# The first transfer of x in two column pieces, each row tile rounded by itself

## The chip, the core and the metric

The kernel runs on one core of one Trainium2 chip. The metric is the device time of one execution, in microseconds (us). The kernel before takes 770.45 us (median of three runs, 770.39 to 770.49).

## The reference, cut to what matters

The layer normalises x (256 tokens by 2048), multiplies it with one wide input projection, runs two attention branches, gates and merges them, projects the result and adds x. Only the first step bears on the change:

```python
def rms_norm(x, gain, eps=NORM_EPS):
    xf = x.astype(jnp.float32)
    y = xf * lax.rsqrt(jnp.mean(xf * xf, axis=-1, keepdims=True) + eps)
    return (y * gain.astype(jnp.float32)).astype(x.dtype)

for l in range(DEPTH):
    h = rms_norm(x, norm_gain[l])
    proj = jnp.einsum('bsd,dn->bsn', h, w_in[l])
    (qa, ka, va, ga, qi, ki, wi, qb, kb, vb, gb, ma, mb) = jnp.split(proj, offsets, axis=-1)
    ...
    merged = jax.nn.sigmoid(ma) * ya + jax.nn.sigmoid(mb) * yb
    x = x + jnp.einsum('bsd,de->bse', merged, w_out[l])
```

`apply_rope` turns the heads by angles, which are the token positions times 64 fixed frequencies.

## The kernel before

**Split products.** Every float32 operand of a matmul is taken as two parts: `hi`, the value rounded to the matmul format (fp32r), and `lo`, the value minus `hi`. A product is three matmuls: hi by hi, lo by hi and hi by lo.

**x.** The program gets x also as `x_columns`, which is x transposed, 128 features to a k-tile, 16 k-tiles of 256 tokens (two row tiles of 128). Ahead of the tiles stand the norm gains (16 columns, `gainT`) and the rotary frequencies (64 columns, `freq`). The SBUF tile `xt` holds all of it. `hT_hi` is x times gain, rounded; `hT_lo` is what is left. In `hT_lo` the rounded columns 64 to 255 of a k-tile are kept once more for packed matmuls (`x_hi_again`, line 1015).

**Units.** Weights are streamed: a unit is two k-tiles of one column chunk, 512 columns wide at most, in a ring of four slots (`raw`, `hi`, `lo`). SyncE (SP) issues the loads, ScalarE (ACT) makes `hi`, VectorE (DVE) makes `lo`, TensorE (PE) multiplies. From unit 4 on, SP waits before a load until DVE has made the `lo` of the unit four places before (line 497 waits, line 499 issues), since the slot is free then. The first three units (`EARLY = 3`) are loaded and split in two halves j = 0 and j = 1, one k-tile each; `FIRST_UNITS` gives the order of the first 24: unit 0 is 336 columns wide, units 1 to 4 are 512, unit 5 is 336.

**The start.** The order of each engine is written out by hand. ACT issues the first transfer of `xt` (line 1003: gains, frequencies and k-tile 0, 336 columns), then loads its function table, rounds the weights of unit 0, rounds columns 64 to 255 of k-tile 0 once more (line 1015, after `x_landed[0]`), and goes on with units 1 and 2 (line 1020). SP issues meanwhile six loads of weights and the next k-tile of x (lines 490 and 482). DVE waits for `x_landed[0]`, makes `hT_hi` of k-tile 0 (line 1453), its `hT_lo` (line 1323), and then the `lo` of the weights (line 1463 for halves, line 1332 for whole units). PE runs 14 matmul records of zeros as a warm-up (line 810). Its real work starts in `rounded_part`: hi by `hT_hi` for the second row tile (line 774) and, in unit 0, for the first (line 776), then by `hT_lo` (lines 778, 780, 784); `low_part` adds `lo` by `hT_hi` (lines 794, 795). Units 1 and 2 use packed rows in place of line 776, which take part of the first row tile. GpSimd (POOL) needs `freq` and the positions to make the rotary angles.

The semaphores of the start are `x_landed[0]` (the transfer), `x_hi_first`, `x_lo_first` and `x_again_first` (k-tile 0 rounded, its rest, its second copy), `hi_first` and `lo_first` (weights, half j = 0), and `hi_ready`, `lo_ready` (half j = 1 and all later units).

Of the kernel before, what the change touches and what calls it, by code (L numbers as in the profile page):

```python
# [30 lines left out]
P = 128  # L31
D = 2048
S = 256
LAST_PIECES = ((0, slice(0, 512)), (1, slice(0, 256)), (1, slice(256, 512)))
RT = S // P
KT = D // P
HD = 128
# [9 lines left out]
BLOCK = 32  # L47
X_CUTS = (0, 1, 2, 4, 6, 8, 10, 12, 14, 16)
X_FRONT = KT + HD // 2
EARLY = 3  # L50
SINES_AT = 12
X_OWN_AFTER = ((3, 2), (3, 4), (3, 6), (4, 0))
# [123 lines left out]
def chunk_bank(c):  # L176

    return {0: 0, 1: 2, 2: 6, 3: 4, 4: 2, 6: 4}.get(c, 2 * ((c + 1) % 2)) if isinstance(c, int) else 2 * ((c + 1) % 2)


def build_layer(nc, x, x_columns, positions, w_in, a_q_gain, a_k_gain, b_q_gain, b_k_gain,
# [4 lines left out]
    with ExitStack() as ctx:  # L186
        place = [-(-nc.sbuf_base // 64) * 64]

        def sb(name, shape, dt=F32, at=None):

            size = 4
            for n in shape[1:]:
                size *= n
            offset = place[0] if at is None else at
            if at is None:
                place[0] += -(-size // 64) * 64
                assert place[0] <= nc.sbuf_usable_end, (name, place[0])
            return nc.alloc_sbuf_tensor_at(name, shape, dt, offset=offset)

        def sem(name):  # L200
            return ctx.enter_context(nc.semaphore(name))
# [6 lines left out]
        hT_hi = sb("hT_hi", [P, KT, S], F32R)  # L208
# [4 lines left out]
        def lo_rows(k, r):  # L213
            return hT_lo[:, k, r * LO_STEP:r * LO_STEP + P]
# [24 lines left out]
        m = sb("m", [P, RT, 2 * D])  # L239
        m_r = sb("m_r", [P, RT, 2 * D], F32R, at=m_at)  # L240
        xt = sb("xt", [P, X_FRONT + KT * S], at=m_at)
        gainT, freq = xt[:, 0:KT], xt[:, KT:X_FRONT]

# [16 lines left out]
            return QK_GAINS[n - C_QK] % 2 == 0  # L262

        def x_tile(k):
            return xt[:, X_FRONT + k * S:X_FRONT + (k + 1) * S]

# [152 lines left out]
        T0, S0 = 4, 6  # L421


        x_landed = [sem(f"x_landed_{i}") for i in range(len(X_CUTS) - 1)]
        phases_landed = sem("phases_landed")
        consts_landed = sem("consts_landed")
# [9 lines left out]
        hi_ready, lo_ready, unit_done = sem("hi_ready"), sem("lo_ready"), sem("unit_done")  # L436
        raw_first = [sem(f"raw_first_{i}") for i in range(EARLY)]
        hi_first, lo_first = sem("hi_first"), sem("lo_first")
        x_hi_first, x_lo_first, x_again_first = sem("x_hi_first"), sem("x_lo_first"), sem("x_again_first")
# [39 lines left out]
        def _(sp):  # L479
            def load_x(j):  # L480
                at = slice(X_FRONT + X_CUTS[j] * S, X_FRONT + X_CUTS[j + 1] * S)
                sp.dma_start(xt[:, at], x_columns[:, at]).then_inc(x_landed[j], 16)
# [5 lines left out]
            def load_first(u, j):  # L488
                c, i = FIRST_UNITS[u]
                sp.dma_start(raw[:, u, j, 0:FIRST_W[c]],  # L490
                             w_in[0][(2 * i + j) * P:(2 * i + j + 1) * P, FIRST_COLS[c]:FIRST_COLS[c] + FIRST_W[c]]
                             ).then_inc((raw_first[u], raw_landed[u])[j], 16)

            def load(slot, u, weights, k0, col, width=CW):

                if not isinstance(u, int) or u >= RING:
                    sp.wait_ge(lo_ready, u - (RING - 1))
                src = weights[0][k0 * P:(k0 + 2) * P, bass.ds(col, width)].rearrange("(k p) n -> p k n", p=P)
                sp.dma_start(raw[:, slot, :, 0:width], src).then_inc(raw_landed[slot], 16)
# [17 lines left out]
            for j in range(2):  # L517
                if j == 1:
                    load_x(1)
                for u in range(EARLY):  # L520
                    load_first(u, j)
            for u in range(EARLY, 3 * CK):
                c, i = FIRST_UNITS[u]
                if c == 0:
                    load_x(i + 1)
                load(u % RING, u, w_in, 2 * i, FIRST_COLS[c], FIRST_W[c])
                if u == EARLY + 1:
                    sp.dma_start(pos_i[:, :], positions).then_inc(phases_landed, 16)
# [219 lines left out]
        def _(pe):  # L748
# [16 lines left out]
            def rounded_part(u, j):  # L765

                c, unit_k = FIRST_UNITS[u]
                k, bank, width = 2 * unit_k + j, chunk_bank(c), FIRST_W[c]
                o_0, o_1 = ps[:, bank, 0:width], ps[:, bank + 1, 0:width]
                w_hi = hi[:, u % RING, j, 0:width]  # L770
                first = k == 0
                pe.wait_ge(hi_first if j == 0 and u < EARLY else hi_ready, u + 1)
                pe.wait_ge(x_hi_first if k == 0 else split_hi, unit_k + 1)
                mm(o_1, hT_hi[:, k, P:S], w_hi, start=first, stop=False)  # L774
                if c >= PACKED:
                    mm(o_0, hT_hi[:, k, 0:P], w_hi, start=first, stop=False)  # L776
                pe.wait_ge(x_lo_first if k == 0 else split_lo, unit_k + 1)
                mm(o_1, lo_rows(k, 1), w_hi, start=False, stop=False)  # L778
                if c >= PACKED:
                    mm(o_0, lo_rows(k, 0), w_hi, start=False, stop=False)  # L780
                else:
                    if k == 0:
                        pe.wait_ge(x_again_first, 1)
                    mm(o_0, packed_rows(k), w_hi, start=first, stop=False)  # L784

            def low_part(u, j):
# [5 lines left out]
                last = k == KT - 1  # L792
                pe.wait_ge(lo_first if j == 0 and u < EARLY else lo_ready, u + 1)
                mm(o_1, hT_hi[:, k, P:S], w_lo, start=False, stop=last)  # L794
# [204 lines left out]
        @block.scalar  # L999
        def _(act):  # L1000
            activation = nc.scalar.activation
            at = slice(0, X_FRONT + X_CUTS[1] * S)
            act.dma_start(xt[:, at], x_columns[:, at]).then_inc(x_landed[0], 16)

            def x_hi(t):
                for j in range(len(X_CUTS) - 1):
# [10 lines left out]
            def early_hi(u, j):  # L1017
                act.wait_ge((raw_first[u], raw_landed[u])[j], 16)
                width = FIRST_W[FIRST_UNITS[u][0]]
                activation(hi[:, u, j, 0:width], raw[:, u, j, 0:width],  # L1020
                           ACT.Copy).then_inc((hi_first, hi_ready)[j], 1)
# [114 lines left out]
                ins.then_inc(indexT_ready, 1)  # L1136

            early_hi(0, 0)
            act.wait_ge(x_landed[0], 16)
            x_hi_again(0).then_inc(x_again_first, 1)  # L1140
            for u in range(1, EARLY):
# [15 lines left out]
            for c in range(2, C_V):  # L1157
                for i in range(CK - RING if c == 2 else 0, CK):
                    at = c * CK + i
# [42 lines left out]
            for c in range(C_V, C_O):  # L1202
                for i in range(CK):
                    u = c * CK + i
                    if i == 0:
                        if c == C_V:
                            qk_group(C_QK + QK_GROUPS - 1)
                        elif c <= C_G:
                            at = (c - 1 - C_V) * CW
                            chunk_to(c - 1, lambda r: v[:, r, at:at + CW])  # L1210
                        elif c <= C_M:
                            at = (c - 1 - C_G) * CW
                            chunk_to(c - 1, lambda r: g[:, r, at:at + CW], ACT.Silu)
                        else:


                            at = (c - 1 - C_M) * CW
# [84 lines left out]
            at = slice(3 * CW + cols.start, 3 * CW + cols.stop)  # L1302
# [5 lines left out]
        def _(dve):  # L1308
            tt, stt, ts = nc.vector.tensor_tensor, nc.vector.scalar_tensor_tensor, nc.vector.tensor_scalar
# [139 lines left out]
                    ins = tt(by_blocks(of_four(n, part, m_r)), columns_of(r), rounded, ALU.subtract)  # L1449
                ins.then_inc(qk_lo_ready, 1)  # L1450

            dve.wait_ge(x_landed[0], 16)
            ts(hT_hi[:, 0, :], x_tile(0), gainT[:, 0:1], None, ALU.mult).then_inc(x_hi_first, 1)  # L1453
            dve.wait_ge(x_hi_first, 1)
            x_lo_tile(0).then_inc(x_lo_first, 1)
            for j in range(2):
                if j == 1:
# [12 lines left out]
            for c in range(2, C_V):  # L1470
                for i in range(CK - RING if c == 2 else 0, CK):
                    at = c * CK + i
# [105 lines left out]
            for c in range(C_V, C_O):  # L1578
                for i in range(CK):
# [46 lines left out]
                    if u in VB_LO:  # L1626
                        n = VB_LO.index(u)
                        at = slice(n * CW, (n + 1) * CW)
# [36 lines left out]
                    if U_B + 8 <= u < U_OGT + 8:  # L1665
# [5 lines left out]
                        if step == (6 if h == B_HEADS - 1 else 7):  # L1671
# [3 lines left out]
                            for t in range(RT):  # L1675
                                at = A_W + h * 2 * HD
# [114 lines left out]
```

## Time and profile before

| what | value |
|---|---|
| median of the runs | 770.45 us |
| the profiled execution's own time | 770.51 us |
| its span | 768.7 us |
| PE busy | 764.8 us, 99% of the span |
| DVE busy | 516.9 us, 67% |
| ACT busy | 431.1 us, 56% |
| granted TensorE clock | full in all 40 slices |
| DMA | 176.80 MB, mean 230 GB/s |

The span runs from the first to the last instruction; 1.8 us of the execution lie outside it. A busy PE says that matmuls follow one another; weight loads for it (PEld) run beside them. "Idle before" is the time in which an engine did nothing ahead of an instruction, and the name behind the arrow is what ended that.

### The profile page before, as it was taken

Reading aid. Unit: us, or ns where it says so; the run is one execution under the profiler, and the core shown is the slowest. Engines: PE = TensorE matmul, PEld = TensorE weight load, DVE = VectorE, ACT = ScalarE, POOL = GpSimd, SP = SyncE. Lnnn points to the kernel's source line nnn. Section 1 sums busy time; section 2 is a strip of 40 time slices with the busy share of each in tenths; the row PEclk is TensorE's granted clock in tenths of the full one; section 3 lists DMA queues with packets and bytes.
Section 4 is the critical chain, followed back from the end, with each engine's and each line's share of the span. In section 5 each row is a group of like instructions: output and inputs, shape, how many; then the busy total and the mean of one; then the engine's idle time right before and its main releaser. Section 6 shows DMA issues by size and latency. Waiting matters only on the chain.

```text
span 768.7 us, 10429 instructions
## 1 busy us (share of the span) xinstructions
PE 764.8 (99%) x3568; PEld 643.8 (84%) x3568; DVE 516.9 (67%) x724; ACT 431.1 (56%) x710; POOL 135.8 (18%) x225
## 2 busy tenths in 40 slices
PE   9999999999999999999999999999999999999998
PEld 8899988888888888888888888888888888888887
DVE  6768788888776755678656665767465567765553
ACT  6855756676663745555656565455576334444331
POOL 4412533322221000000212222312110011110000
PEclk9999999999999999999999999999999999999999
DMA  8988889998888675666866768767767888887553
GB/s 294 318 258 276 264 245 291 276 254 266 245 245 243 187 200 167 193 192 172 240 207 197 222 192 270 234 185 222 224 208 224 302 230 240 246 242 230 198 183 122
DMA packets 89612, 176.80 MB, mean 230 GB/s; under 512 B 7616, under 2 KB 15424, under 8 KB 89312
## 3 DMA queue, kind: packets, MB, share of 16 engines
q1 hardware_dynamic: 80752, 152.06, 65.8%
q0 software_dynamic: 8528, 23.87, 10.9%
q8 instruction: 25, 0.41, 0.2%
q10 hardware_dynamic: 288, 0.30, 0.1%
q14 instruction: 19, 0.16, 0.1%
HBM read 162.18 MB, written 14.02 MB: 229 GB/s over the span
## 4 chain that ended last, share of the span: by engine, by line
PE 99%; DMA 0%; DVE 0%; issue 0%
PE ps L760 29%; PE ps L762 29%; PE ps L761 29%; PE ps L774 1%; PE ps L778 1%; PE ps L794 1%; PE ps L795 1%; PE ps L784 1%; PE ps L860 0%; PE ps L963 0%; PE ps L962 0%; PE ps L961 0%; DMA xt<-in_x_columns 0%; PE ps L780 0%; PE ps L776 0%; PE ps L861 0%
## 5 line engine op out<-in xcount | busy, mean ns | idle before, releaser
L1332 DVE TENSOR_TENSOR lo<-raw,hi 128x1024 fp32r<-128x1024 f32 (+2 forms) x277 | 331.2, 1202 | 230.1 <-ACT hi L1041 229.3
L1041 ACT ACTIVATE hi<-raw 128x1024 fp32r<-128x1024 f32 (+2 forms) x277 | 286.3, 1038 | 291.5 <-PE ps L762 254.7
L760 PE MATMUL ps<-hi,hT_hi 128*128 128x512 f32 (+1 forms) x880 | 339.9, 386 | 0.0
L761 PE MATMUL ps<-lo,hT_hi 128*128 128x512 f32 (+1 forms) x880 | 339.0, 385 | 0.0
L762 PE MATMUL ps<-hi,hT_lo 128*128 128x512 f32 (+1 forms) x880 | 339.0, 385 | 0.0
L762 PEld LDWEIGHTS ps<-hi,hT_lo 128*128 128x128 f32 x880 | 165.2, 188 | 32.1
L760 PEld LDWEIGHTS ps<-hi,hT_hi 128*128 128x128 f32 x880 | 165.2, 188 | 31.5
L761 PEld LDWEIGHTS ps<-lo,hT_hi 128*128 128x128 f32 x880 | 165.2, 188 | 31.3
L760 PE MATMUL ps<-hi,ogT_hi 128*128 128x512 f32 x128 | 49.8, 389 | 0.0
L761 PE MATMUL ps<-lo,ogT_hi 128*128 128x512 f32 x128 | 49.8, 389 | 0.0
L762 PE MATMUL ps<-hi,ogT_lo 128*128 128x512 f32 x128 | 49.8, 389 | 0.0
L704 POOL DMA_DIRECT2D probs<-work x12 | 6.8, 567 | 173.3 <-DVE work L1536 173.3
L711 POOL DMA_DIRECT2D work<-probs x48 | 26.1, 550 | 53.1 <-DMA probs<-work 53.1
L761 PEld LDWEIGHTS ps<-lo,ogT_hi 128*128 128x128 f32 x128 | 24.0, 188 | 5.0
L760 PEld LDWEIGHTS ps<-hi,ogT_hi 128*128 128x128 f32 x128 | 24.0, 188 | 5.0
L762 PEld LDWEIGHTS ps<-hi,ogT_lo 128*128 128x128 f32 x128 | 24.0, 188 | 5.0
L688 POOL DMA_DIRECT2D v<-turned x32 | 17.5, 554 | 28.4 <-DMA turned<-swapped 24.7
L1182 ACT ACTIVATE work<-work,small 128x128 f32<-128x128 f32 (+1 forms) x32 | 14.3, 447 | 13.4 <-DVE small L1507 13.4
L1102 ACT ACTIVATE roped<-stage 128x128 f32<-128x128 f32 x64 | 18.9, 296 | 0.3
L774 PE MATMUL ps<-hi,hT_hi 128*128 128x512 f32 (+1 forms) x48 | 17.7, 369 | 0.3 <-DVE hT_hi L1453 0.3
L604 POOL TENSOR_TENSOR small<-small,half 128x8 f32<-128x8 f32 (+1 forms) x13 | 17.8, 1369 | 1.1
L738 POOL DMA_DIRECT2D turned<-swapped x4 | 2.2, 559 | 88.1 <-DVE swapped L1718 88.1
(199 smaller groups left out, 665.1 us busy)
## 6 DMA issues: line engine op xcount, KB each, us to landing
raw<-in_w_in SPq DMA_DIRECT2D x190, 512.0 KB, 4.5
raw<-in_w_out SPq DMA_DIRECT2D x32, 512.0 KB, 4.2
raw<-in_w_o_a SPq DMA_DIRECT2D x16, 512.0 KB, 5.9
raw<-in_w_o_b SPq DMA_DIRECT2D x16, 512.0 KB, 4.2
raw<-in_w_in SPq DMA_DIRECT2D x16, 384.0 KB, 4.9
turned<-swapped POOLq DMA_DIRECT2D x12, 512.0 KB, 3.3
v<-turned POOLq DMA_DIRECT2D x32, 128.0 KB, 5.8
raw<-in_w_in SPq DMA_DIRECT2D x7, 336.0 KB, 4.6
```

Of the source, the lines that this page charges most:

```text
L604: return tt(out, mean, half[:, 0:width], ALU.pow)
L688: pool.dma_start(to.rearrange("j (q n) -> j q n", q=P // BLOCK), turned_rows[c]).then_inc(turned_back, 16)
L711: pool.dma_start(to.rearrange("j (q n) -> j q n", q=P // BLOCK), rows[c]).then_inc(probs_back, 16)
L760: mm(o, a_hi, w_hi[:, j], start=first and j == 0, stop=False)
L761: mm(o, a_hi, w_lo[:, j], start=False, stop=False)
L762: ins = mm(o, a_lo, w_hi[:, j], start=False, stop=j == 1 and last)
L774: mm(o_1, hT_hi[:, k, P:S], w_hi, start=first, stop=False)
L778: mm(o_1, lo_rows(k, 1), w_hi, start=False, stop=False)
L1041: activation(hi[:, slot, :, 0:width], raw[:, slot, :, 0:width], ACT.Copy).then_inc(hi_ready, 1)
L1102: ins = activation(roped[:, r, at], stage[:, r, at], ACT.Square, accum_out=ss_h[:, j:j + 1])
L1182: ins = activation(probs[buf][:, at], masked[buf][:, at], ACT.Exp, scale=SCALE, bias=neg_max[:, j:j + 1], accum_out=sum_p[:, j:j + 1])
L1332: tt(lo[:, slot, :, 0:width], raw[:, slot, :, 0:width], hi[:, slot, :, 0:width].bitcast(F32), ALU.subtract).then_inc(lo_ready, 1)
```

## The change

The layout of `x_columns` becomes: frequencies (64 columns), k-tile 0 (256 columns), gains (16 columns), then the other k-tiles at the places they had. ACT now issues two transfers in place of one. Each piece has a semaphore of its own, `x_half_landed` for the second row tile (columns 192 to 319) with the gains (320 to 335), and `x_landed[0]` for the frequencies (0 to 63) with the first row tile (64 to 191). `X_HALF = 192` is where they meet. The piece with the second row tile is issued first; it is 144 columns (72 KB), the other 192 columns (96 KB).

DVE rounds k-tile 0 in two instructions of 128 columns, each after its own piece, and goes on with `hT_lo` when both are done. PE waits for the first before line 774's matmul and for both before line 776's. ACT waits for both before its second rounding. POOL waits for `x_landed[0]` as before.

```diff
+X_FIRST = HD // 2
+X_HALF = X_FIRST + P
...
-        gainT, freq = xt[:, 0:KT], xt[:, KT:X_FRONT]
+        gainT, freq = xt[:, X_FIRST + S:X_FRONT + S], xt[:, 0:X_FIRST]
...
         def x_tile(k):
-            return xt[:, X_FRONT + k * S:X_FRONT + (k + 1) * S]
+            first = X_FIRST if k == 0 else X_FRONT + k * S
+            return xt[:, first:first + S]
...
+        x_half_landed = sem("x_half_landed")
...
                 if c >= PACKED:
+                    if k == 0:
+                        pe.wait_ge(x_hi_first, 2)
                     mm(o_0, hT_hi[:, k, 0:P], w_hi, start=first, stop=False)
...
-            at = slice(0, X_FRONT + X_CUTS[1] * S)
-            act.dma_start(xt[:, at], x_columns[:, at]).then_inc(x_landed[0], 16)
+            for at, landed in ((slice(X_HALF, X_FRONT + S), x_half_landed), (slice(0, X_HALF), x_landed[0])):
+                act.dma_start(xt[:, at], x_columns[:, at]).then_inc(landed, 16)
...
             early_hi(0, 0)
+            act.wait_ge(x_half_landed, 16)
             act.wait_ge(x_landed[0], 16)
             x_hi_again(0).then_inc(x_again_first, 1)
...
-            dve.wait_ge(x_landed[0], 16)
-            ts(hT_hi[:, 0, :], x_tile(0), gainT[:, 0:1], None, ALU.mult).then_inc(x_hi_first, 1)
-            dve.wait_ge(x_hi_first, 1)
+            for rows, landed in ((slice(P, S), x_half_landed), (slice(0, P), x_landed[0])):
+                dve.wait_ge(landed, 16)
+                ts(hT_hi[:, 0, rows], x_tile(0)[:, rows], gainT[:, 0:1], None, ALU.mult).then_inc(x_hi_first, 1)
+            dve.wait_ge(x_hi_first, 2)
             x_lo_tile(0).then_inc(x_lo_first, 1)
...
-    x_columns = _np.concatenate([_np.asarray(inputs["norm_gain"])[0].reshape(KT, P).T,
-                                 _np.broadcast_to(freqs, (P, HD // 2)),
-                                 _np.asarray(inputs["x"])[0].T.reshape(KT, P, S).transpose(1, 0, 2).reshape(P, KT * S)],
-                                axis=1)
+    x_tiles = _np.asarray(inputs["x"])[0].T.reshape(KT, P, S).transpose(1, 0, 2).reshape(P, KT * S)
+    x_columns = _np.concatenate([_np.broadcast_to(freqs, (P, HD // 2)), x_tiles[:, 0:S],
+                                 _np.asarray(inputs["norm_gain"])[0].reshape(KT, P).T, x_tiles[:, S:]], axis=1)
```

The start of ACT's own program before, where `xt` is x with gains and frequencies, `hi` and `raw` the weights rounded and as loaded:

```order
L1003 DMA xt<-in_x_columns 128x336
L1020 ACT_TABLE_LOAD
L1020 ACTIVATE hi<-raw 128x336 [waits raw_first_0]
L1015 ACTIVATE hT_lo<-xt 128x64 [waits x_landed_0]
L1020 ACTIVATE hi<-raw 128x512 [waits raw_first_1]
```

And of the changed kernel, the same place:

```order
L1011 DMA xt<-in_x_columns 128x144
L1011 DMA xt<-in_x_columns 128x192
L1028 ACT_TABLE_LOAD
L1028 ACTIVATE hi<-raw 128x336 [waits raw_first_0]
L1023 ACTIVATE hT_lo<-xt 128x64 [waits x_landed_0,x_half_landed]
L1028 ACTIVATE hi<-raw 128x512 [waits raw_first_1]
```

One issue stands more ahead of the table load, and the second rounding of x waits for both pieces; nothing else has moved.

The start of DVE's program before, where `hT_hi` and `hT_lo` are the two parts of x and `lo` the rest of the weights:

```order
L1453 TENSOR_SCALAR hT_hi<-xt 128x256 [waits x_landed_0]
L1323 SCALAR_TENSOR_TENSOR hT_lo<-xt,hT_hi 128x2x128 [waits x_hi_first]
L1463 TENSOR_TENSOR lo<-raw,hi 128x336 [waits hi_first]
L1463 TENSOR_TENSOR lo<-raw,hi 128x512 [waits hi_first] x2
L1323 SCALAR_TENSOR_TENSOR hT_lo<-xt,hT_hi 128x2x128 [waits split_hi]
```

And of the changed kernel:

```order
L1463 TENSOR_SCALAR hT_hi<-xt 128x128 [waits x_half_landed]
L1463 TENSOR_SCALAR hT_hi<-xt 128x128 [waits x_landed_0]
L1332 SCALAR_TENSOR_TENSOR hT_lo<-xt,hT_hi 128x2x128 [waits x_hi_first]
L1473 TENSOR_TENSOR lo<-raw,hi 128x336 [waits hi_first]
L1473 TENSOR_TENSOR lo<-raw,hi 128x512 [waits hi_first] x2
L1332 SCALAR_TENSOR_TENSOR hT_lo<-xt,hT_hi 128x2x128 [waits split_hi]
```

The rounding of k-tile 0 is cut in two, and what follows has its place and its waits as before.

## Rows read from the trace of the kernel before

**Rows 1.** The page: busy us, share of the span and instructions of each engine.
```profile
PE 764.8 (99%) x3568; PEld 643.8 (84%) x3568; DVE 516.9 (67%) x724; ACT 431.1 (56%) x710; POOL 135.8 (18%) x225
```

**Rows 2.** Waits in the whole span: engine, line, releaser, total us, times, longest.
```profile
PEld ps L774 <- ACT hi L1041: 0.5, 1, 0.5
```

**Rows 3.** Chain of waits, 0 to 6 us: start, length, what.
```profile
0.74 3.11 DMA xt<-in_x_columns
...
3.88 0.36 DVE hT_hi L1453
4.24 0.14 issue
4.38 0.43 PE ps L774
```

**Rows 4.** Timeline of ACT, ACTq being its DMA issues: start, length, instruction.
```profile
0.74 0.40 ACTq L1003 DMA_DIRECT2D xt<-in_x_columns  x1
...
3.68 0.48 ACT L1020 ACTIVATE hi<-raw 128x336 fp32r<-128x336 f32 x1 [1.22 <-DMA raw<-in_w_in]
4.07 0.33 ACT L1015 ACTIVATE hT_lo<-xt 128x64 fp32r<-128x64 f32 x1
4.46 1.30 ACT L1020 ACTIVATE hi<-raw 128x512 fp32r<-128x512 f32 x2
...
12.50 1.06 ACT L1041 ACTIVATE hi<-raw 128x1024 fp32r<-128x1024 f32 x1 [1.74 <-DMA raw<-in_w_in]
```

**Rows 5.** Timeline of DVE, 3 to 7.3 us.
```profile
4.26 0.49 DVE L1323 SCALAR_TENSOR_TENSOR hT_lo<-xt,hT_hi 128x256 fp32r<-128x256 f32 x1
4.67 0.50 DVE L1463 TENSOR_TENSOR lo<-raw,hi 128x336 fp32r<-128x336 f32 x1
...
5.12 1.36 DVE L1463 TENSOR_TENSOR lo<-raw,hi 128x512 fp32r<-128x512 f32 x2
...
5.79 0.69 DVE L1463 TENSOR_TENSOR lo<-raw,hi 128x512 fp32r<-128x512 f32 x1
...
6.84 0.50 DVE L1463 TENSOR_TENSOR lo<-raw,hi 128x336 fp32r<-128x336 f32 x1
```

**Rows 6.** Timeline of PE around 13.4 us.
```profile
12.96 0.39 PE L794 MATMUL ps<-lo,hT_hi 128*128 128x512 f32 x1
13.19 0.39 PE L795 MATMUL ps<-lo,hT_lo 128*128 128x512 f32 x1
13.62 0.50 PE L774 MATMUL ps<-hi,hT_hi 128*128 128x512 f32 x1
13.96 0.40 PE L778 MATMUL ps<-hi,hT_lo 128*128 128x512 f32 x1
```

**Rows 7.** DMA issues between 0 and 0.9 us: KB each, us to landing.
```profile
raw<-in_w_in SPq DMA_DIRECT2D x1, 168.0 KB, 2.9
```

**Rows 8.** The same, issues between 1.5 and 2.9 us.
```profile
raw<-in_w_in SPq DMA_DIRECT2D x2, 256.0 KB, 3.3
...
raw<-in_w_in SPq DMA_DIRECT2D x1, 168.0 KB, 3.3
```

**Rows 9.** SP's timeline, and unit 4's time to landing.
```profile
2.60 1.38 SPq L490 DMA_DIRECT2D raw<-in_w_in  x3
...
7.37 0.38 SPq L499 DMA_DIRECT2D raw<-in_w_in  x1
...
raw<-in_w_in SPq DMA_DIRECT2D x1, 512.0 KB, 5.1
```

**Rows 10.** DMA queues, 2 to 4 us: packets, MB, share of 16 engines.
```profile
q1 hardware_dynamic: 289, 0.46, 66.2%
q10 hardware_dynamic: 144, 0.17, 25.5%
```

**Rows 11.** Stretches: us; busy PE, PEld, DVE, ACT, POOL; clock, DMA share, GB/s.
```profile
10.00:12.00 2.00, 2.00 (x10) 1.67 (x9) 1.93 (x3) 0.76 (x1) 0.00 (x0) 1.00 0.95 302
...
14.00:244.00 230.00, 230.00 (x1087) 198.15 (x1086) 182.95 (x230) 150.13 (x308) 72.56 (x104) 1.00 0.89 265
```

## The prediction

> **What bounds the kernel now.** I began with the page's first part. PE is busy 764.8 of 768.7 us [rows 1], so only time in which PE waits can be won or lost, unless its own work changes, and no matmul is added or taken away. The second view is that of the waits over the whole span. For PE it has, besides a pause ahead of the index scores that no engine ends, only places in the first 14 us: line 774's first matmul waits for DVE's `hT_hi`, and a later weight load of the same line, for unit 4, waits for ACT's `hi` [rows 2]. The table of stretches says the same: from 14 to 244 us PE is busy 230.00 of 230.00 us at the full granted clock [rows 11]. So whatever the change does must reach past 14 us, or it is gone.
>
> The third view, the chain of waits, shows the first place: the transfer of x is issued at 0.74 and lands 3.11 us later at 3.85, DVE rounds it until 4.24, and PE starts at 4.38 [rows 3]. The timeline of PE shows the second: matmuls follow one another by 0.23 us (12.96 to 13.19), so the next was due at 13.42, but the next starts at 13.62 and its follower only at 13.96, 0.34 behind instead of 0.23 [rows 6]. That is 0.20 us idle plus 0.11 us of restart. ACT explains it: its `hi` of unit 4 began at 12.50 after 1.74 us of waiting for the weights, and took 1.06 [rows 4]. Those weights were issued at 7.37 and landed 5.1 us later [rows 9]. This second place is the bound that counts. A start of PE that comes earlier makes it wait longer there, and a start up to 0.20 us later is swallowed there.
>
> **When the two pieces land.** The whole 168 KB took 3.11 us. SP's 168 KB of the same moment took 2.9, its 256 KB 3.3 [rows 7, 8]. That is 0.4 us for 88 KB, 0.0045 us per KB. The first piece (72 KB, 96 less) then takes 3.11 - 0.44 = 2.67 us from 0.74 and lands at 3.41. The second is issued one issue later; an issue takes 0.40 us [rows 4], with the gap to the next some 0.43, so at 1.17. It has 96 KB (72 less): 3.11 - 0.33 = 2.78 us, landing at 3.95. Bounds: were time proportional to bytes it would be 1.17 + 3.11 x 96/168 = 2.95; at the slower early load's 3.3 us, 4.47 [rows 8]. I take 3.95, since two early loads of different size give the slope. So the second piece lands about 0.10 us later than the whole did.
>
> **DVE, part by part.** Before, it began at 3.88, and `hT_lo` at 4.26. The first rounding now runs from 3.44 and is over before the second piece is there. For 128 columns no row exists: 336 columns take 0.50 and 512 take 0.69 [rows 5], 0.0011 us per column, so the cut of 128 takes 0.14 off the 0.36 of 256 columns [rows 3], which leaves 0.22 (bounds: half of 0.36, 0.18; all of it, 0.36). Then: 3.95 + 0.03 + 0.22 + 0.03 = 4.23 for the start of `hT_lo`, 0.03 earlier than 4.26. With the bounds of the rounding it is 4.19 to 4.37.
>
> Does a gain there go on? `lo` of unit 0 would start at 4.64 instead of 4.67. But `lo` of unit 1 starts at 5.12 [rows 5], and the `hi` it needs comes from ACT: rounding at 4.46, two of 512 in 1.30 us, so the first is over at about 5.10 [rows 4]. ACT's chain from 3.68 has no idle time up to there and begins with the landing of unit 0's weights. The second `lo` of this kind, at 5.79, stands right behind ACT's end at 4.46 + 1.30 = 5.76. From there DVE goes on to `lo` of unit 0's second half, 6.84 to 7.34, which lets SP issue unit 4 at 7.37 [rows 5, 9]. So ACT carries the date of unit 4, and an earlier DVE start is worth nothing.
>
> **ACT.** The second issue moves ACT's table load back by 0.43. The 1.22 us wait for weights that ended at 3.68 [rows 4] hides it; uncovered it would cost the 0.43. At 4.07 ACT needs both pieces: free if the second lands by 4.04. DVE, by the sum above, tolerates 4.02. Both margins over 3.95 are about 0.08 us; a landing L later than that moves ACT, DVE and the issue of unit 4 by L - 4.03. At 4.47 that is 0.44.
>
> **PE.** The first matmul needs the second row tile (3.44 + 0.22 = 3.66) and `hi` of unit 0, ready at 3.68 + 0.48 = 4.16, which is the later. With the 0.14 between release and start [rows 3] it starts at 4.30, 0.08 earlier than 4.38. The added wait ahead of line 776 (both roundings, 4.20) is met by then. Behind it stand the `hT_lo` matmuls, that need DVE's 4.23 + 0.49, and the low part, that needs 5.14: there the gain is down to 0.03 us, and at 13.42 it is nothing. If the added wait does hold, the whole in-order queue of PE stands behind it, again with 0.20 us of cover. Had the 0.08 survived to the end, 770.4 would be the time.
>
> **POOL and SP.** POOL needs `freq` only together with the positions, which SP issues after unit 4's weights, at over 7.37 us [rows 9]: nothing. No issue of SP is moved.
>
> **More packets.** The x queue had 144 packets in its 25.5% of 2 us x 16 engines, 57 ns each at 1.2 KB; the other queue 289 in 66.2%, 73 ns at 1.6 KB [rows 10]. The line through both gives 11 ns without bytes. A second transfer adds as many packets as one has, 144: 144 x 11 / 16 = 0.10 us for each engine (bounds: none, or all 57 ns fixed, 0.51). The engines are the bound until unit 4 lands, but not wholly: their share is 0.95 between 10 and 12 us [rows 11]. I take half, 0.05 us, on the landing of unit 4, and from there to the end, as PE never waits again.
>
> **The sum.** PE's start -0.08, of which 0 is left; unit 4's issue 0; its landing +0.05. The profiled execution would go from 770.51 to 770.56, 0.06 above the median, so the forecast is 770.5 us.
>
> **Two rules weighed.** The transfer's time against its size is 3.11 us for 168 KB here. The Trainium skill (DMA: Bandwidth & Descriptors, Anatomy of one DMA — SWDGE (gpsimd) path) gives about 2.0 us fixed and the bytes over 436 GB/s, measured on POOL's path. By the slope of that rule the second piece saves 0.17 us and lands at 1.17 + 2.94 = 4.11, over the threshold: an estimate of +0.08 us, where the rows give 0. On the order between queues, both show bytes in the same 2 us, in shares 25.5 and 66.2% [rows 10]. The same page (Queues, rings and completion order) says that an engine takes turns between queues, packet by packet; the trace agrees, and it speaks against the third rival.
>
> **The rivals.**
> 1. *Fixed cost per transfer (a little slower).* If 96 KB take nearly what 168 KB took, the second piece lands at up to 1.17 + 3.11 = 4.28: 0.25 us late for ACT and DVE, unit 4 issued at 7.62. It decides from 4.03. With the packets 770.45 + 0.25 + 0.05 = 770.75. For it: 168 KB issued later by SP took 3.3 us, no less than 256 KB [rows 8]. Against: it ran among more traffic.
> 2. *Weights earlier (a little faster).* 96 of the 168 KB of x come 0.43 us later, so unit 0's weights meet less company; 98 thousand bytes at the 0.63 MB in 2 us seen there [rows 10] are 0.31 us. ACT could start at 3.37, but its second instruction waits for 3.95 + 0.03 and not 4.07: 0.09 of it is left, and 0.07 after DVE. Time 770.4.
> 3. *The second piece behind SP's loads (slower).* SP issues two loads of 256 KB and one of x right behind its first, and the second halves from 2.60 on [rows 9]. If the second piece is served only after all up to the first of those, it lands with that, at 2.60 + 3.3 = 5.90 [rows 8]: 5.90 - 4.03 = 1.87 us on ACT, DVE and unit 4, which carries it past PE's cover. Time 772.3. A change that can be measured needs a landing past 5.57.
> 4. *It does not do what it says.* The halves are there one by one, but PE's first matmul waits for `hi` of unit 0. That is inside the forecast.
>
> **How the numbers follow.** Forecast 0.62, rival 1 0.18, rival 2 0.14, rival 3 0.03, anything not named 0.03. A difference under 0.2%, 1.54 us, can't be told from no change here. Only rival 3 is past it, and half of the unnamed on either side: faster 0.02, within 0.2% 0.94, slower 0.04. The range takes in rivals 1 and 2, the packets' upper bound (0.51) and some tenths for transfers that interleave otherwise: 770.1 to 771.0.
>
> **What would show it.** Two transfers on ACT's queue, landing near 3.4 and 3.95; DVE's `hT_lo` between 4.19 and 4.30; PE's first matmul near 4.30, waiting for ACT and not for DVE; the idle time near 13.4 still there, 0.20 to 0.3 us; unit 4's `hi` between 12.4 and 12.7; PE without idle time after it. I am wrong if PE's wait at 13.4 vanishes, if the landing of unit 4 moves by over 0.3 us, or if the second piece lands after 4.3.

## The result, and the profile after

The changed kernel takes 772.17 us (median of 22 runs, 770.71 to 773.22), the kernel before, run beside it, 770.43 us (22 runs, 770.15 to 771.61). The ratio of the two, taken over all runs and not from the medians (these alone give 1.0023), is 1.0017, 95% interval 1.0011 to 1.0023: slower, by more than the measurement is uncertain and by about 0.2%. In the experiments below, too, the ratio stands beside the median and is not worked out from it. The median of 772.17 lies outside the predicted range of 770.1 to 771.0.

The times of the changed kernel are two groups with nothing between 771.33 and 772.09: 8 runs at 770.71 to 771.33 and 14 at 772.09 to 773.22. Of the kernel before 21 of 22 are at or under 770.94. The profiled execution, 772.63 us with a span of 770.8, is one of the upper group, and so is the median; of the lower group no execution was profiled.

The page has PE 2.2 us busier, with the same number of matmuls, which answers to [rows 1]; part 3 has 432 packets on the queue of x's first transfer, where before it has 288:

```profile
PE 767.0 (99%) x3568; PEld 645.9 (84%) x3568; DVE 517.2 (67%) x725; ACT 431.2 (56%) x710; POOL 135.8 (18%) x225
...
q10 hardware_dynamic: 432, 0.30, 0.1%
```

PE does the same work and needs longer for it. The waits of PE and PEld in the whole span (engine, line, releaser, total us, times, longest) have changed place against [rows 2]; the wait for unit 4's weights is gone, and those that another engine ends are all in the first 6 us:

```profile
PE ps L784 <- DVE hT_hi L1463: 0.3, 1, 0.3
...
PEld ps L784 <- DVE hT_hi L1463: 0.7, 1, 0.7
...
PEld ps L786 <- DVE hT_lo L1332: 0.2, 1, 0.2
PEld ps L780 <- ACT hi L1028: 0.2, 1, 0.2
```

The chain of waits up to 7 us (start, length, what) answers to [rows 3]. The second piece is issued at 1.18, lands 3.46 us later, at 4.64, and PE's second matmul starts at 5.00:

```profile
0.74 0.41 ACTq L1011
...
1.18 3.46 DMA xt<-in_x_columns
...
4.66 0.30 DVE hT_hi L1463
...
5.00 0.65 PE ps L784
5.65 0.52 PE ps L786
```

DVE's first rounding starts when the first piece is there, near 3.6. ACT starts on unit 0's weights earlier than in [rows 4] and then waits for the second piece of x:

```profile
3.61 0.28 DVE L1463 TENSOR_SCALAR hT_hi<-xt 128x128 fp32r<-128x128 f32 x1 [3.61 <-DMA xt<-in_x_columns]
```

```profile
3.42 0.48 ACT L1028 ACTIVATE hi<-raw 128x336 fp32r<-128x336 f32 x1 [0.48 <-DMA raw<-in_w_in]
4.72 0.35 ACT L1023 ACTIVATE hT_lo<-xt 128x64 fp32r<-128x64 f32 x1 [0.82 <-DMA xt<-in_x_columns]
```

The timeline of PE has the loss itself:

```profile
4.04 0.62 PE L780 MATMUL ps<-hi,hT_hi 128*128 128x336 f32 x1
5.00 0.65 PE L784 MATMUL ps<-hi,hT_hi 128*128 128x336 f32 x1 [0.35 <-DVE hT_hi L1463]
...
6.25 0.48 PE L802 MATMUL ps<-lo,hT_hi 128*128 128x336 f32 x1
6.53 0.48 PE L803 MATMUL ps<-lo,hT_hi 128*128 128x336 f32 x1
6.81 0.63 PE L780 MATMUL ps<-hi,hT_hi 128*128 128x512 f32 x1
7.24 0.63 PE L786 MATMUL ps<-hi,hT_lo 128*128 128x512 f32 x1
...
8.94 0.63 PE L780 MATMUL ps<-hi,hT_hi 128*128 128x512 f32 x1
9.37 0.53 PE L786 MATMUL ps<-hi,hT_lo 128*128 128x512 f32 x1
9.74 0.40 PE L792 MATMUL ps<-hi,hT_lo 128*128 128x512 f32 x1
...
10.43 0.32 PE L780 MATMUL ps<-hi,hT_hi 128*128 128x336 f32 x1
...
16.14 0.39 PE L786 MATMUL ps<-hi,hT_lo 128*128 128x512 f32 x1
```

Read the distances between starts. Matmuls of 336 columns follow by 0.28 us and those of 512 by 0.43, that is 1.2 columns per ns, the lower of TensorE's two levels (1.2 GHz). From 9.74 on those of 512 follow by 0.23, 2.2 columns per ns, the upper level (2.4 GHz). The matmul at 9.37, with 0.53 us between the 0.63 of one level and the 0.40 of the other, is where the pace rose. The kernel before does its 512-column matmuls 0.23 apart from the first one on, and the short 0.31 us of its second matmul, at 4.64, say that it has the upper level by then:

```profile
4.64 0.31 PE L776 MATMUL ps<-hi,hT_hi 128*128 128x336 f32 x1
...
5.64 0.39 PE L774 MATMUL ps<-hi,hT_hi 128*128 128x512 f32 x1
5.87 0.40 PE L778 MATMUL ps<-hi,hT_lo 128*128 128x512 f32 x1
...
6.80 0.39 PE L774 MATMUL ps<-hi,hT_hi 128*128 128x512 f32 x1
...
7.93 0.31 PE L774 MATMUL ps<-hi,hT_hi 128*128 128x336 f32 x1
```

The ledger follows from these two timelines. PE's second matmul is 0.36 us late (5.00 against 4.64), unit 1's first 1.17 (6.81 against 5.64), unit 2's first 2.14 (8.94 against 6.80), unit 0's second half 2.50 (10.43 against 7.93). Then the pace is equal, and at unit 4 the idle time and restart of [rows 6] are not there any more, which gives 0.32 back: its second matmul is at 16.14 instead of 13.96, 2.18 late. The span is 2.1 us longer.

The column of granted clock does not tell this. It says 1.00 in both kernels for 5.00 to 9.30 us. The count in brackets behind PE's busy time does: 22 matmuls that fall at least in part into that stretch before, and 11 after. First before, then after (columns as in [rows 11]):

```profile
5.00:9.30 4.30, 4.30 (x22) 3.70 (x22) 3.70 (x7) 3.79 (x10) 0.00 (x0) 1.00 1.06 358
```

```profile
5.00:9.30 4.30, 4.30 (x11) 3.57 (x12) 4.11 (x8) 3.79 (x10) 0.00 (x0) 1.00 1.02 349
```

The load of unit 4, which the prediction took for the bound, was issued later and landed earlier, against [rows 9] and [rows 4]. SP's issue, its time to landing and ACT's rounding of it:

```profile
7.93 0.38 SPq L505 DMA_DIRECT2D raw<-in_w_in  x1
...
raw<-in_w_in SPq DMA_DIRECT2D x1, 512.0 KB, 3.6
```

```profile
11.61 1.06 ACT L1049 ACTIVATE hi<-raw 128x1024 fp32r<-128x1024 f32 x1 [0.48 <-DMA raw<-in_w_in]
```

### The profile page after: what moved, and what is told of

It reads as the page before. It is cut to its first block, busy times and chain, and to the rows that moved or that the text cites. A ratio compares the mean times of both kernels' runs of the same rounds, so it can differ in the third digit from the quotient of the medians.

```text
span 770.8 us, 10432 instructions
## 1 busy us (share of the span) xinstructions
PE 767.0 (99%) x3568; PEld 645.9 (84%) x3568; DVE 517.2 (67%) x725; ACT 431.2 (56%) x710; POOL 135.8 (18%) x225
## 4 chain that ended last, share of the span: by engine, by line
PE 99%; DMA 0%; DVE 0%; ACTq 0%; issue 0%
PE ps L766 29%; PE ps L767 29%; PE ps L768 29%; PE ps L786 1%; PE ps L802 1%; PE ps L803 1%; PE ps L780 1%; PE ps L792 1%; PE ps L868 0%; DMA xt<-in_x_columns 0%; PE ps L969 0%; PE ps L971 0%; PE ps L970 0%; PE ps L784 0%; PE ps L788 0%; PE ps L869 0%
## 5 line engine op out<-in xcount | busy, mean ns | idle before, releaser
L768 PE MATMUL ps<-hi,hT_lo 128*128 128x512 f32 (+1 forms) x880 | 339.1, 385 | 0.0
L1191 ACT ACTIVATE work<-work,small 128x128 f32<-128x128 f32 (+1 forms) x32 | 14.2, 446 | 13.4 <-DVE small L1517 13.4
L786 PE MATMUL ps<-hi,hT_lo 128*128 128x512 f32 (+1 forms) x48 | 18.3, 381 | 0.0
```

Source lines behind the costliest of these rows:

```text
L768: ins = mm(o, a_lo, w_hi[:, j], start=False, stop=j == 1 and last)
L1191: ins = activation(probs[buf][:, at], masked[buf][:, at], ACT.Exp, scale=SCALE, bias=neg_max[:, j:j + 1], accum_out=sum_p[:, j:j + 1])
```

## The experiments

Two theories stood at the start. **A**: zeros end at 4.10 us, and PE then has too little work, one lone matmul until 5.0; the rise of its pace to the upper level, which else comes about then, stays out until 9.4 to 9.7, and the slow matmuls are the loss. **B**: the second piece is late and delays DVE, ACT and the load of unit 4; the pace has no part in it. All kernels ran beside the kernel before, in three sets: its median was 770.52 us beside the first four, 770.46 beside the next four and 770.60 beside the last three.

**More warm-up in the changed kernel.**

```diff
-WARM_UP = 7
+WARM_UP = 9
```

> The changed kernel with 9 zero matmuls (18 records) of warm-up in place of 7, so that zeros run until about 5.06 us instead of 4.10. Theory A (PE's idle time behind the warm-up keeps the matmuls of 4.0 to 9.4 us at 1.2 GHz, and these slow matmuls are the loss): the first real matmuls run at 2.4 GHz (336 columns 0.15 us apart), the second mode of the times is gone, 770.4 to 770.9 us. Theory B (the late second piece delays DVE, ACT and the load of unit 4, the clock plays no part): the landing stays late, 771.7 us or more, since PE starts no earlier.

Measured: 770.87 us (770.67 to 773.16, 11 runs; ratio 1.0010, 1.0001 to 1.0019), one run above 771.44. The second piece was still late, at 4.5, and PE's weight loads waited 0.4 us for its rounding and 0.3 us for `hT_lo`, but the real matmuls ran at the upper level. The zero records start 0.2 us apart up to 4.10 and the last two of them 0.11 to 0.12 apart, so the pace rose while the zeros ran, about 0.2 us ahead of the first real matmul:

```profile
3.68 0.92 PE L818 MATMUL ps<-const-float32-0.0 128*128 128x128 f32 x5
4.36 0.40 PE L780 MATMUL ps<-hi,hT_hi 128*128 128x336 f32 x1
4.88 0.42 PE L784 MATMUL ps<-hi,hT_hi 128*128 128x336 f32 x1
...
6.24 0.39 PE L780 MATMUL ps<-hi,hT_hi 128*128 128x512 f32 x1
6.47 0.40 PE L786 MATMUL ps<-hi,hT_lo 128*128 128x512 f32 x1
```

1.3 of the 1.7 us between the medians went with two more zero matmuls and no other edit. A holds. What is left, 0.35 us over the 770.52 of the kernel before beside it, is the most that B alone is worth.

**Less warm-up in the kernel before.**

```diff
-WARM_UP = 7
+WARM_UP = 5
```

> The kernel before, one transfer, with 5 zero matmuls of warm-up, so that zeros end near 3.15 us and PE idles some 1.2 us before 4.38. Nothing is late but the warm-up. Theory A: slow matmuls at the start in most executions, 772 us or more. Theory B: no change, 770.4 us.

Measured: 772.64 us (771.70 to 773.39, 7 runs; ratio 1.0026, 1.0014 to 1.0037). Nothing in it is late but the end of the zeros. x landed at 3.9 as before, and PE had 14 matmuls in the stretch from 5.00 to 9.30 where the kernel before has 22:

```profile
4.42 0.62 PE L774 MATMUL ps<-hi,hT_hi 128*128 128x336 f32 x1 [1.17 <-DVE hT_hi L1453]
...
9.64 0.63 PE L794 MATMUL ps<-lo,hT_hi 128*128 128x512 f32 x1
10.07 0.58 PE L795 MATMUL ps<-lo,hT_lo 128*128 128x512 f32 x1
10.49 0.31 PE L774 MATMUL ps<-hi,hT_hi 128*128 128x336 f32 x1
```

**The transfer split, the rounding not.**

```diff
-            for rows, landed in ((slice(P, S), x_half_landed), (slice(0, P), x_landed[0])):
-                dve.wait_ge(landed, 16)
-                ts(hT_hi[:, 0, rows], x_tile(0)[:, rows], gainT[:, 0:1], None, ALU.mult).then_inc(x_hi_first, 1)
-            dve.wait_ge(x_hi_first, 2)
+            dve.wait_ge(x_half_landed, 16)
+            dve.wait_ge(x_landed[0], 16)
+            ts(hT_hi[:, 0, :], x_tile(0), gainT[:, 0:1], None, ALU.mult).then_inc(x_hi_first, 1)
+            dve.wait_ge(x_hi_first, 1)
...
-                    if k == 0:
-                        pe.wait_ge(x_hi_first, 2)
```

> The changed kernel with its two transfers, but DVE waits for both and rounds k-tile 0 in one instruction of 256 columns, and PE has no added wait. Theory A and B: the second piece still lands near 4.6, so PE starts near 5.1 with idle time behind the warm-up: 772 us or a little more, no better than the change. If instead the early lone matmul of the changed kernel at 4.04 is what spoils the clock, it is back at 770.5.

Measured: 772.35 us (770.89 to 773.18, 11 runs; ratio 1.0017, 1.0008 to 1.0026), four runs at 770.89 to 771.02 and seven from 771.94 on. The same two groups without the lone matmul, so that one is not what spoils the pace.

**The rounding split, the transfer not.**

```diff
-            for at, landed in ((slice(X_HALF, X_FRONT + S), x_half_landed), (slice(0, X_HALF), x_landed[0])):
-                act.dma_start(xt[:, at], x_columns[:, at]).then_inc(landed, 16)
+            at = slice(0, X_FRONT + S)
+            act.dma_start(xt[:, at], x_columns[:, at]).then_inc(x_landed[0], 16)
...
-            act.wait_ge(x_half_landed, 16)
...
-            for rows, landed in ((slice(P, S), x_half_landed), (slice(0, P), x_landed[0])):
+            for rows, landed in ((slice(P, S), x_landed[0]), (slice(0, P), x_landed[0])):
```

> The changed kernel with its layout, its two roundings and PE's added wait, but one transfer of 336 columns as before. If the transfer is the whole cause (A and B): 770.5 us, as before. If the cut rounding or the added wait of PE costs: 772 us.

Measured: 770.52 us (770.33 to 770.99, 11 runs; ratio 1.0001, 0.9992 to 1.0010). Two roundings, PE's added wait and the new layout cost nothing that shows. The second transfer is the cause. The wait for unit 4's weights is there again, as in the kernel before. In this profile the first real matmuls run at the lower level and the pace rises near 5.4, yet the time is that of the kernel before: by this profile a rise that is 0.8 us late is covered by PE's wait near 13.4.

```profile
4.36 0.62 PE L779 MATMUL ps<-hi,hT_hi 128*128 128x336 f32 x1 [0.26 <-DVE hT_hi L1461]
```

**Work in the gap.** This leaves the transfers, the waits and the seven zeros ahead as they are.

```diff
                     if k == 0:
+                        if u == 0:
+                            for _ in range(2):
+                                mm(ps[:, 3, 0:P], zeros, zeros, start=True, stop=True)
                         pe.wait_ge(x_hi_first, 2)
```

> The changed kernel as it is, with two zero matmuls (into an unused bank of PSUM) put between unit 0's first matmul and its second, so that PE has work while it would wait for the second piece. The transfers, the roundings and every wait stay. Theory A (idle time ahead of the rise of PE's pace): the rise comes before or soon after 5 us in nearly all executions, 770.5 to 771.0 us. Rival C (the total of warm-up work ahead of the first real matmul, 7 matmuls, is what counts): no help, 772 us in most.

Measured: 770.89 us (770.68 to 771.40, 11 runs; ratio 1.0006, 0.9997 to 1.0015), no run in an upper group. The rise came while the zeros ran; the matmul behind them, at 5.09, has the short duration of the upper level:

```profile
4.06 0.62 PE L780 MATMUL ps<-hi,hT_hi 128*128 128x336 f32 x1
4.48 0.85 PE L785 MATMUL ps<-const-float32-0.0 128*128 128x128 f32 x4
5.09 0.40 PE L787 MATMUL ps<-hi,hT_hi 128*128 128x336 f32 x1
...
14.28 0.39 PE L789 MATMUL ps<-hi,hT_lo 128*128 128x512 f32 x1
```

So in these runs the work may stand in the gap as well as ahead of it, and rival C, by which only work ahead of the first real matmul counts, is out. The last row is unit 4's second matmul: 14.28 against 13.96 in [rows 6]. These 0.32 us are the price of the late piece without the pace.

**A longer idle time, and nothing late.**

```diff
-WARM_UP = 7
+WARM_UP = 6
```

> The kernel before with 6 zero matmuls: zeros end near 3.67 us, so PE idles about 0.7 us, as long as in the changed kernel, but with everything landed at the old times. Theory A: a mix of executions near 770.5 and near 772.3, the slow ones a third to two thirds. Theory B (lateness of the second piece): no change.

Measured: 771.76 us (770.34 to 772.52, 11 runs; ratio 1.0015, 1.0006 to 1.0024), one run at 770.34 and ten from 771.64 on. In the profile PE idles 0.77 us ahead of line 774 and works at the lower level until 8.8 to 9.2:

```profile
4.44 0.62 PE L774 MATMUL ps<-hi,hT_hi 128*128 128x336 f32 x1 [0.77 <-DVE hT_hi L1453]
...
8.82 0.51 PE L778 MATMUL ps<-hi,hT_lo 128*128 128x512 f32 x1
```

With nothing late the pace alone costs 1.3 us, which B can't give. The share of executions in the upper group was higher than A had it, ten of eleven where a third to two thirds were expected. "As long as in the changed kernel" holds only roughly: there the row of PE's second matmul shows 0.35 us of idle time, or 0.7 us if the lone matmul ahead of it is counted by its 0.28 us at the lower level and not by the end that the profile gives it.

**One transfer, issued second.**

```diff
+        x_gain_landed = sem("x_gain_landed")
...
+            act.dma_start(xt[:, 0:4], x_columns[:, 0:4]).then_inc(x_gain_landed, 16)
+            at = slice(4, X_FRONT + X_CUTS[1] * S)
             act.dma_start(xt[:, at], x_columns[:, at]).then_inc(x_landed[0], 16)
...
+            act.wait_ge(x_gain_landed, 16)
...
+            dve.wait_ge(x_gain_landed, 16)
             dve.wait_ge(x_landed[0], 16)
```

> The kernel before, with the transfer of x in one piece but for four gain columns (2 KB), which are a transfer of their own ahead of it. The large piece is issued at 1.17 instead of 0.74. If the time from issue to landing hardly depends on the size (96 KB took 3.3 to 3.5 us, 168 KB 3.1), it lands at 4.3 to 4.6, and PE idles 0.7 to 1 us: a mix of 770.7 and 772.5 us. If the size counts as predicted, and the second piece of the change was late for another reason, about 4.3.

Measured: 773.32 us (770.99 to 774.28, 5 runs; ratio 1.0038, 1.0024 to 1.0052). The runs but one are at 773.14 or more. The issues up to 1.5 us, KB and us to landing, and PE's first real matmul:

```profile
xt<-in_x_columns ACTq DMA_DIRECT2D x1, 166.0 KB, 3.5
xt<-in_x_columns ACTq DMA_DIRECT2D x1, 2.0 KB, 2.5
```

```profile
5.24 0.39 PE L775 MATMUL ps<-hi,hT_hi 128*128 128x336 f32 x1 [1.14 <-DVE hT_hi L1458]
```

166 KB issued at 1.18 take as long as the 96 KB of the change, and 0.4 us longer than 168 KB issued at 0.74; even 2 KB took 2.5 us. Whether the 0.4 us come from the place in ACT's queue or from what SP's loads move at that moment, this kernel can't tell, since both changed. The profiled execution is the one run at 770.99: PE idled 1.14 us there and yet worked at the upper level from its first real matmul, at 5.24. So idle time makes a late rise likely, not certain. The time of this one execution, 0.5 us over the kernel before, is what x landing 0.8 to 0.9 us late costs with the pace at the upper level.

**The kernel before with 8 zeros.**

```diff
-WARM_UP = 7
+WARM_UP = 8
```

> The kernel before with 8 zero matmuls, which end near 4.58 at the low pace. PE has no idle time before its first real matmul. Theory A: the few executions of before that are above 770.9 are gone; median 770.4 us, within 0.1 of before, since the idle time near 13.4 us swallows 0.2 us of a later start. Theory B: 770.5 to 770.7.

Measured: 770.47 us (770.22 to 770.90, 11 runs; ratio 0.9999, 0.9990 to 1.0008). No gain in the median. None of its 11 runs is above 770.90; of the 27 runs of the kernel before beside it four are, one of them, at 772.03, in an upper group. Too few to call them gone. In its profile the first real matmul is at 4.45 at the lower level, the pace rises near 5.8, and the time is still that of the kernel before.

**The second piece on SP's queue, ahead of the weights.**

```diff
-            for at, landed in ((slice(X_HALF, X_FRONT + S), x_half_landed), (slice(0, X_HALF), x_landed[0])):
-                act.dma_start(xt[:, at], x_columns[:, at]).then_inc(landed, 16)
+            at = slice(X_HALF, X_FRONT + S)
+            act.dma_start(xt[:, at], x_columns[:, at]).then_inc(x_half_landed, 16)
...
+            at = slice(0, X_HALF)
+            sp.dma_start(xt[:, at], x_columns[:, at]).then_inc(x_landed[0], 16)
             for j in range(2):
```

> The changed kernel with the second piece issued by SP at 0.74, ahead of its weights, instead of by ACT at 1.18. If lateness comes from being the second issue of its queue, both pieces land by 3.6; but unit 0's weights are now SP's second issue and land near 4.1 to 4.3, so PE's first matmul starts near 4.6 to 4.8, behind 0.5 to 0.7 us of idle time. Theory A: a mix again, slow executions in a third to two thirds, 771 to 772 us. If only a late x mattered (B): 770.5 us.

Measured: 771.58 us (771.10 to 772.72, 11 runs; ratio 1.0013, 1.0004 to 1.0022), eight runs up to 771.67 and three from 772.48 on. Each piece is the first of its queue, and both are fast:

```profile
xt<-in_x_columns SPq DMA_DIRECT2D x1, 96.0 KB, 2.4
xt<-in_x_columns ACTq DMA_DIRECT2D x1, 72.0 KB, 2.2
```

In the changed kernel the same 72 KB, also issued at 0.74 as the first of ACT's queue, took 0.6 us longer:

```profile
xt<-in_x_columns ACTq DMA_DIRECT2D x1, 72.0 KB, 2.8
```

So the place in the queue is not all of it. What differs for this piece is what runs beside it: here the other piece of x and weights issued 0.45 us later, there SP's 168 KB of weights, issued at the same time.

The price is on the weights, all of which SP issues 0.45 us later. PE waits for `hi` of three units in turn, 1.6 us of weight-load waits:

```profile
PEld ps L782 <- ACT hi L1030: 1.6, 3, 0.6
```

**The same with 8 zeros.** The edit is that above with `WARM_UP = 8`.

> The same with 8 zero matmuls, ending near 4.58: no idle time ahead of the first real matmul. Theory A: no slow executions, 770.4 to 770.8 us. Theory B: like the one with 7. A version that could match or beat the kernel before; by the idle time at 13.4 us, which bounds it, not by over 0.2 us.

Measured: 771.18 us (770.87 to 771.97, 11 runs; ratio 1.0007, 0.9999 to 1.0016). No run is near the 772.48 and more of three runs with 7 zeros, but the median is above what A expected. I had counted only the first weights as late, and in the profile the real matmuls run at the lower level until 5.7 at least. It does not beat the kernel before.

**The changed kernel with 8 zeros.** The edit is `WARM_UP = 8`.

> The changed kernel with 8 zero matmuls: PE has work until 4.58, then the lone matmul of the second row tile until about 4.75, then waits for the second piece until 5.0, 0.25 us as in the kernel before. Theory A: nearly no slow executions, 770.6 to 770.9 us. If only work past 5 us helped, a mix of 770.8 and 772.3.

Measured: 770.88 us (770.71 to 773.13, 12 runs; ratio 1.0006, 0.9997 to 1.0014), one run of twelve in the upper group. In its profile the rise came near 6.5 us, later than in the kernels with 9 zeros or with work in the gap, and the span is 769.4.

## Why the prediction was wrong

**The bound was read right, its condition was not.** That only PE's time counts and that all that can change lies at the start held: from 16 to 244 us PE is busy 228.00 of 228.00 us in the profile after. The step that failed is "unless its own work changes, and no matmul is added or taken away": it took the pace of PE's matmuls as fixed, and so put at nothing, without a reason, the term that cost most. The same matmuls took nearly twice as long from 5.0 to 9.4 us (0.43 us from one to the next and not 0.23), about 1.5 us of the total in 14 of 22 executions. I had read the granted clock of 1.00 as the pace, and no rival had a pace in it. A look at distances would have shown that the zeros of the warm-up, 0.21 us apart in the kernel before, are at the lower level (with nine zeros the last of them are 0.11 to 0.12 apart), and that the real work has the upper one by its second matmul, at 4.64. The rise falls just where the change works. The Trainium skill (TensorE: Matmul & The Clock Gate, What's actually happening) says that the throttled state is the default and that activity releases it, and (What you observe) that the moment varies from run to run. The traces agree with the first: zeros ahead of the real work or in the gap brought the rise forward. Of the second they show that two kernels with the same start on PE differ: it came by 4.6 us in the kernel before and near 5.4 with one transfer and the rounding split. After the change it came at 9.4 to 9.7. It is a page I should have weighed before a change to what PE does between the warm-up and its work.

**When the pieces land.** The first was put at 3.41 and came near 3.6. The second was put at 3.95 with bounds 2.95 and 4.47, and came at 4.64, outside them. The step was the slope of 0.0045 us per KB, drawn through two loads of SP that also differ in when they were issued; the bounds came from the same loads. Place in the queue, time of issue and company together outweigh size here: 96 KB took 2.4 us as the first of SP's queue and 3.3 to 3.5 as the second of ACT's, 166 KB took 3.5 in the same second place, and 72 KB took 2.8 or 2.2 us as the first of ACT's, with SP's weights issued at the same time or 0.45 us later. No run separates the three. The slope of the Trainium skill's rule (DMA: Bandwidth & Descriptors, Anatomy of one DMA — SWDGE (gpsimd) path), which I weighed and set aside, gave 4.11, an estimate that is nearer and still 0.5 early.

**DVE.** 128 columns took 0.28 to 0.29 us and not 0.22, inside the bounds. With 0.35 for 256 columns the second 128 add only 0.06 to 0.07, so by these two sizes about 0.22 us don't depend on the columns (an estimate). It did not matter beside the landing. The threshold of 4.02 for DVE does not follow from the sum: `hT_lo` is 0.03 early at a landing of 3.95, which gives 3.98. Beside 4.64 that is small.

**ACT.** A threshold near 4.04 was right in kind: ACT waited 0.82 us for x and went on at 4.72. The table load stayed hidden, but with less room than said, 0.48 us, as ACT started on unit 0's weights at 3.42 and not 3.68. That is the size of rival 2's mechanism, 0.26 us where it had 0.31, and worth nothing since x was late. With nearly all of x issued later (one transfer, issued second) ACT started on them at 3.10, which speaks for it too.

**PE.** Its first matmul started at 4.04 and not 4.30, waiting for ACT as forecast. The added wait did hold, for 0.7 us of weight-load time, and "again with 0.20 us of cover" was the whole price I gave it. Cover for lateness is right: where the pace rose early in most runs, the change with fill or more zeros was 0.28 to 0.43 us above before, and the profile with fill has 0.32 at unit 4 (0.6 late, 0.3 swallowed at 13.4). The prediction's own formula with the measured landing gives as much: 4.64 - 4.03 = 0.61, less 0.20 of cover, 0.41. Rival 1 had 0.30 for its smaller lateness, with no cover taken off.

**Rival 3.** Its time of 772.3 is near the measured 772.17 by luck. It has the second piece at 5.90 behind SP's loads; the piece landed at 4.64, and with that landing 1.3 of the 1.7 us went away when only zeros were added.

**Unit 4.** That a late piece would move its issue was right: 0.56 us, where the formula with 4.64 gives 0.61. That its landing hangs on its issue was wrong. It landed 0.9 us earlier, 3.6 us after issue instead of 5.1. In the other kernels it took 3.6 to 4.2 us where x was late and 4.1 to 5.0 where it was on time, and no run was made to find out why. That the idle time at 13.4 would still be there was wrong because these weights were there in time, and because PE came later.

**Packets.** 144 more, as counted. The line through the two rows gives 9 ns and not 11, which changes nothing: the 0.05 us can't be told apart in any run.

**The sum, put right.** The second landing at 4.64 costs 0.3 to 0.4 us behind PE's cover: the middle of the lower group, 770.8, is 0.4 above the kernel before. It also leaves PE with one matmul between 4.1 and 5.0 us, and in 14 of 22 executions 1.5 us more are lost (the middle of the upper group is 772.3), in the profiled one by some 4.4 us of work at the lower level. Both parts together, 0.4 and 14/22 of 1.5, are 1.35 us, and the means of all runs differ by 1.36. Of the change as it is, no execution of the lower group was profiled; that it has the upper level early is read from the kernels with more zeros.

**What stays open.** What decides in one execution whether the rise comes in time. By the idle time that PE's row shows ahead of the real work, 0.77 us with six zeros went with the upper group in ten of eleven runs, 1.17 us with five zeros in all seven, 0.98 us with seven zeros (the rounding not split) in only seven of eleven, and 1.14 us with seven zeros did not prevent the upper level in the one profiled, though the other four of its runs are at 773.14 or more. So the length of the idle time alone does not order them; how much work stood ahead of it may count too, and no run separates the two.

## What to carry to other kernels

A start that overlaps a warm-up with the first loads is one unit: whatever makes the first loads later by some tenths can cost several times that through the pace of the first matmuls, so look whether the warm-up reaches to the latest landing before trying to shorten it. Here more zeros took back most of the loss but did not beat the kernel before. Do not split the one transfer that PE waits for on one queue without a measurement; here the second issue cost 0.43 us and landed as late after it as a transfer nearly twice its size did. Read PE's pace from the distances of equal matmuls, and look at all runs and not at a median when a kernel's times fall in two groups.

## What the runs showed of the hardware

- The granted clock of the profile was 1.00 while matmuls of 512 columns ran 0.43 us apart (the changed kernel, 6.8 to 9.4 us), and 1.00 when they ran 0.23 apart (the kernel before).
- A transfer's time to landing depended on more than its size: 96 KB took 2.4 us as the first of SP's queue and 3.3 to 3.5 us behind another on ACT's; 72 KB as the first of ACT's took 2.2 us, and 2.8 beside 168 KB of weights issued at the same time.
- Two zero matmuls in the gap were as good for the pace as two more ahead of the real work: no run of 11 in the upper group, and one of 11.
- A load of 512 KB issued 0.56 us later landed 0.9 us earlier (3.6 us after issue against 5.1); why was not tested.
